# Modulation products as plain f32 matmuls on quarters of the array, half of them moved into block two, and an early gating of three retention heads

## The reference

```python
s_c = jax.nn.silu(c)
s_cc = jax.nn.silu(c_ctx)[None]
for i in range(DEPTH):
    ml = (s_c @ w_mod[i] + b_mod[i]).reshape(-1, 3, 3, D)     # for x
    mc = (s_cc @ w_mod[i] + b_mod[i]).reshape(-1, 3, 3, D)    # for the context
    h = gated_residual(h, ml, 0, swiglu(ada_in(h, norm_g[i, 0], ml, 0), ...), 0.5)
    xl = ada_in(h, norm_g[i, 1], ml, 1)      # then retention (i = 0) or neighbourhood attention (i = 1)
    h = gated_residual(h, ml, 1, yl, 1.0)
    h = gated_residual(h, ml, 2, swiglu(ada_in(h, norm_g[i, 2], ml, 2), ...), 0.5)
# ada_in: rms_norm(x) * (1 + m[:, j, 1]) + m[:, j, 0];  gated_residual: h + w * m[:, j, 2] * y
```

## Time and profile before

| | us |
|---|---|
| median of three runs | 3498.28 |
| lowest, highest | 3494.55, 3510.05 |
| the profiled execution, its span | 3498.12, 3496.3 |
| PE busy | 3340.3 (96%) |
| PEld, DVE, ACT, POOL busy | 2800.2, 1829.8, 1416.7, 93.1 |
| moved by DMA | 497.13 MB, 142 GB/s on average |

### The profile page before, as it was taken

One profiled execution on the slowest core, in us unless ns is written; L12 is line 12 of the kernel. 1 busy time (PEld: TensorE's weight loads), 2 busy tenths in 40 slices (PEclk: granted clock), 3 DMA queues, 4 the chain that ended last, 5 costly groups with the idle time before them and its releaser, 6 DMA issues.

```text
span 3496.3 us, 44481 instructions
## 1 busy us (share of the span) xinstructions
PE 3340.3 (96%) x17862; PEld 2800.2 (80%) x17862; DVE 1829.8 (52%) x2656; ACT 1416.7 (41%) x1898; POOL 93.1 (3%) x127
## 2 busy tenths in 40 slices
PE   7999979999999979999999999989999999999998
PEld 6888768888887768878888778768888788887797
DVE  6755666757756767753334343463333433344654
ACT  5644535545545435542222233233221322234543
POOL 0000000000000000000000000000000000021000
PEclk9999989999999989999999999999999999999999
DMA  7854426857754427843232222212333223254254
GB/s 242 275 186 158 151 77 199 266 196 258 254 169 152 135 96 229 265 157 97 97 112 99 85 85 85 84 49 97 97 103 103 87 98 110 91 133 100 76 181 156
DMA packets 354902, 497.13 MB, mean 142 GB/s; under 512 B 12658, under 2 KB 223500, under 8 KB 354700
## 3 DMA queue, kind: packets, MB, share of 16 engines
q1 hardware_dynamic: 351052, 483.76, 42.2%
q0 software_dynamic: 3648, 10.54, 1.4%
HBM read 493.16 MB, written 1.10 MB: 141 GB/s over the span
## 4 chain that ended last, share of the span: by engine, by line
PE 88%; DVE 6%; ACT 2%; issue 2%; POOL 1%; DMA 1%; SPq 0%; DVEq 0%; POOLq 0%; ACTq 0%
PE bank L483 27%; PE bank L484 26%; PE bank L485 26%; PE bank L496 2%; PE bank L498 2%; DVE wlo L1430 1%; PE bank L882 1%; ACT whi L1019 1%; DVE cv L1711 1%; DMA raw<-in_nat_w_qkv_dram 0%; PE bank L616 0%; PE bank L631 0%; POOL small L2174 0%; PE bank L867 0%; POOL small L2179 0%
## 5 line engine op out<-in xcount | busy, mean ns | idle before, releaser
L1430 DVE TENSOR_TENSOR wlo<-raw,whi 128x1024 fp32r<-128x1024 f32 (+1 forms) x926 | 1107.4, 1213 | 1263.4 <-ACT whi L1019 1262.1
L1019 ACT ACTIVATE whi<-raw 128x1024 fp32r<-128x1024 f32 (+1 forms) x926 | 953.3, 1047 | 1249.7 <-PE bank L485 1212.3
L483 PE MATMUL bank<-xTh,whi 128*128 128x256 f32 (+1 forms) x3200 | 1043.5, 326 | 9.4 <-ACT whi L1019 4.1
L484 PE MATMUL bank<-xTl,whi 128*128 128x256 f32 (+1 forms) x3200 | 1039.4, 325 | 0.0
L485 PE MATMUL bank<-xTh,wlo 128*128 128x256 f32 (+1 forms) x3200 | 1039.0, 325 | 0.0
L483 PEld LDWEIGHTS bank<-xTh,whi 128*128 128x128 f32 x3200 | 608.2, 190 | 72.7 <-issue 9.7
L484 PEld LDWEIGHTS bank<-xTl,whi 128*128 128x128 f32 x3200 | 608.4, 190 | 52.4 <-issue 0.5
L485 PEld LDWEIGHTS bank<-xTh,wlo 128*128 128x128 f32 x3200 | 607.8, 190 | 49.0
L483 PE MATMUL bank<-whi,hh 128*128 128x512 f32 x968 | 376.8, 389 | 0.0
L484 PE MATMUL bank<-wlo,hh 128*128 128x512 f32 x968 | 376.6, 389 | 0.0
L485 PE MATMUL bank<-whi,hl 128*128 128x512 f32 x968 | 376.6, 389 | 0.0
(11 more groups left out here) (331 smaller groups left out, 2485.0 us busy)
## 6 DMA issues: line engine op xcount, KB each, us to landing
raw<-in_ffn_w_in_dram SPq DMA_DIRECT2D x176, 1024.0 KB, 5.2
raw<-in_ffn_w_out_dram SPq DMA_DIRECT2D x80, 1024.0 KB, 5.1
raw<-in_w_mod_dram SPq DMA_DIRECT2D x72, 1024.0 KB, 5.2
raw<-in_w_in_dram SPq DMA_DIRECT2D x44, 1024.0 KB, 5.0
raw<-in_ret_w_in_dram SPq DMA_DIRECT2D x24, 1024.0 KB, 5.1
raw<-in_w_branch_dram SPq DMA_DIRECT2D x12, 1024.0 KB, 5.1
raw<-in_nat_w_qkv_dram SPq DMA_DIRECT2D x12, 1024.0 KB, 8.5
raw<-in_ffn_w_out_dram SPq DMA_DIRECT2D x16, 512.0 KB, 3.4
```

The lines of the kernel that those rows point to most:

```text
L483: pe.matmul(ps, lh, rh, start=start, stop=False, skip_group_check=True)
L484: pe.matmul(ps, lh, rl, start=False, stop=False, skip_group_check=True)
L1019: nc.scalar.activation(hi, src, ACT.Copy).then_inc(*e.inc("hi", key, part))
L1430: nc.vector.tensor_tensor(lo, src, hi.bitcast(F32), ALU.subtract).then_inc(*e.inc("lo", key, part))
```

## The change

The slabs of w_mod leave the common order. A new class `Modulation` lays them out: 12 batches of three modulations, six halves each. Each half is loaded as it is into one of four buffers `mraw` and multiplied unsplit, by plain f32 matmuls; each of the four 128-row pieces j of a half goes to columns 32j to 32j + 31 of the array, and so to partitions 32j and on of bank 7. The stationary side is a window of 32 columns of `scp`, which is zero but for two; the window is shifted by two columns for each modulation of a batch, so that a batch of three shares one bank. Six batches (one layer's) are in the FFNs of block one, six in the FFNs g1 and g2 of layer 0 and g1 of layer 1, all with T = 512. Four batches of block one have their last half at the end of the FFN (`END`). A batch's turn is one matmul with `sel` per 128 columns, which sums the four pieces at once. FFNs with modulations use seven banks. ACT copies the rows where DVE did. The gate rows of a layer are made in g1, whose group 9 turns them.

At the end of retention DVE gates and adds the sum of the first three heads beforehand (`three_heads`), and `rows` has only head 3's share left; ACT takes the split that followed `first_squares` ahead of it, DVE takes its own in the norm.

```diff
+MOD_BATCHES = {("f1", 0): (0,), ("f2", 0): (1, 2), ("f1", 1): (3, 4), ("f2", 1): (5,),
+               ("g1", 0): (6, 7), ("g2", 0): (8, 9), ("g1", 1): (10, 11)}
+MOD_POINTS = {1: (9, 13, 17, 21, 25, END), 2: (8, 10, 12, 14, 16, 18, 20, 22, 24, 26, 28, END),
+              512: (2, 3, 4, 5, 6, 7, 9, 9, 10, 11, 12, 13)}
...
+                        if wide:
+                            ahead = 3 if n < NMOD else at - 1
+                        else:
+                            ahead = 28 if at == END else max(6, at - (4 if len(batches) == 1 else 2))
+                        self.loads.setdefault(first + ahead, []).append(q)
...
                     sp.dma_start(view(raw[s % NRAW], key), src).then_inc(landed[s % NRAW], 16)
+                    for q in mods.loads.get(s, ()):
+                        name = mods.halves[q][4]
+                        if q >= NMOD:
+                            sp.wait_ge(*e.at("modk", q - NMOD))
+                        if name not in (("f1", 0), ("f1", 1), ("g1", 0)) and q < mods.first[name] + NMOD:
+                            sp.wait_ge(*e.at("turn", name, KD - 1))
+                        sp.dma_start(mraw[q % NMOD][:, :, :], mods.halves[q][3]).then_inc(mod_landed[q % NMOD], 16)
...
-                for part in range(2):
-                    wh, wl = split_ready(("mod", i, half), part)
-                    for j in range(2):
-                        k = 4 * half + 2 * part + j
-                        pe.matmul(ps[0:4, :], sc4[:, k, :], wh[:, j, :], start=k == 0, stop=False,
-                                  skip_group_check=True)
-                        m = pe.matmul(ps[0:2, :], sc4[:, k, 0:2], wl[:, j, :], start=False, stop=k == KD - 1,
-                                      skip_group_check=True)
...
+                ps = bank[MODS[0]]
+                pe.wait_ge(mod_landed[q % NMOD], 16 * (q // NMOD + 1))
+                for j in range(4):
+                    pm = pe.matmul(ps[32 * j:32 * j + 32, :], scp[:, 4 * half + j, 4 - 2 * m:36 - 2 * m], mraw[q % NMOD][:, j, :],
+                                   start=m == half == 0, stop=m == BATCH - 1 and half == 1, skip_group_check=True)
+                pm.then_inc(*e.inc("modk", q, also=[("modp", b)] if m == BATCH - 1 and half == 1 else []))
...
                 for c in range(4):
-                    m = pe.transpose(ps[:, 4 * c:4 * c + 4], modrow[0:4, c * P:(c + 1) * P], ident[0:4, 0:4])
-                m.then_inc(*e.inc("modtp", i))
+                    m = pe.matmul(ps[:, 6 * c:6 * c + 6], modrow[:, c * P:(c + 1) * P], sel, start=True, stop=True)
+                m.then_inc(*e.inc("modtp", b))
...
+                        mods_at(name, 2 * g + half)
...
+                        mods_at(name, 22 + 6 * n + d)
                 rows_by_tile([(name, "down", 1, d) for d in (4, 5)], ("down", name, 1), ps, *hv, k0, KF)
+                mods_at(name, END)
...
+                    if t == 0 and name in PREVIOUS:
+                        mod_rows(PREVIOUS[name], END)
...
+            def mod_rows(name, at):
+
+                if (name, at + 1) in mods.turns:
+                    b = mods.turns[name, at + 1]
...
+                    act.wait_ge(*e.at("modp", b))
+                    if b:
+                        act.wait_ge(*e.at("modtp", b - 1))
+                    A(modrow[:, :], unit("modp", b)[:, :], ACT.Copy).then_inc(*e.inc("modrow", b, frees=("modp", b)))
...
             ahead(until, ("rw", 3, 0))
+            ahead_of_tail(until, ("rw", 3, 1))
             first_squares(("g2", 0), 512)
-            ahead_of_tail(until, ("rw", 3, 1))
...
+            def gated(t, n, stage, key):
+
+                TT(stripe(X, n, t), stripe(X, n, t), stripe(Y, n, t), ALU.add).then_inc(*e.inc(stage, key, t, n))
+
+            def three_heads(t, n):
+                dve.wait_ge(*e.at("Y", 2, n, t))
+                dve.wait_ge(*e.at("gb", ("r",)))
+                TT(stripe(Y, n, t), stripe(Y, n, t), stripe(gbm, n, t // 2), ALU.mult).then_inc(*e.inc("Yg", 2, n, t))
+                dve.wait_ge(*e.at("Yg", 2, n, t))
+                gated(t, n, "X3", "r")
+
             def rows(t, n=1):
-                row(3, t, n)
-                dve.wait_ge(*e.at("Y", 3, n, t))
-                dve.wait_ge(*e.at("gb", ("r",)))
-                link(TT(stripe(Y, n, t), stripe(Y, n, t), stripe(gbm, n, t // 2), ALU.mult))
-                TT(stripe(X, n, t), stripe(X, n, t), stripe(Y, n, t), ALU.add)\
-                    .then_inc(*e.inc("X", ("g2", 0), t, n))
+                dve.wait_ge(*e.at("rwp", 3, n, t))
+                dve.wait_ge(*e.at("X3", "r", t, n))
+                TT(stripe(Y, n, t), unit("rwp", 3, n, t)[:, :], stripe(gbm, n, t // 2), ALU.mult)\
+                    .then_inc(*e.inc("Yg", 3, n, t, frees=("rwp", 3, n, t)))
+                dve.wait_ge(*e.at("Yg", 3, n, t))
+                gated(t, n, "X", ("g2", 0))
...
+            until(slabs.part_index[("rw", 3, 1), 0])
+            for t in range(4):
+                for n in range(2):
+                    three_heads(t, n)
             ahead(until, ("rw", 3, 0))
             for t in range(4):
                 rows(t, 0)
-            ahead_of_tail(until, ("rw", 3, 1))
             first_squares(("g2", 0), 512)
```

More of the change, by code:

```diff
@@ L135, in add, with __init__ @@
         self.items.append((key, src, kt, n, len(pieces)))
+class Modulation:
+    def __init__(self, slabs, w):
+        self.halves, self.uses, self.loads, self.turns, self.first, self.last = [], {}, {}, {}, {}, {}
+        for name, batches in MOD_BATCHES.items():
+            wide = name[0][0] == "g"
+            points = MOD_POINTS[512 if wide else len(batches)]
+            first = slabs.index[name, "gate", 0]
+            self.first[name], n = len(self.halves), 0
+            for b in batches:
+                for m in range(BATCH):
+                    l, g = divmod(BATCH * b + m, 18)
+                    for half in range(2):
+                        q, at = len(self.halves), points[n]
+                        src = w["w_mod_2"][l][512 * half:512 * half + 512, 512 * g:512 * g + 512]
+                        self.halves.append((b, m, half, src.rearrange("(k p) n -> p k n", p=P), name))
+                        self.uses.setdefault((name, at), []).append(q)
+                        if wide:
[3 more added lines that the diff above has]
+                        self.loads.setdefault(first + ahead, []).append(q)
+                        n += 1
+                self.turns[name, at + 1] = b
+            self.last[name] = len(self.halves) - 1
 def plan(w):
@@ L143, in rows, with ffn @@
         return m[k0 * P:(k0 + kt) * P, c0:c0 + n].rearrange("(k p) n -> p k n", p=P)
[L145 to L149, removed]
+    def ffn(name, w_up, w_down):
         for g in range(GROUPS):
@@ L223, in build @@
     slabs = plan(w)
+    mods = Modulation(slabs, w)
     with ExitStack() as ctx:
@@ L471, in new @@
             def new(*key, ring=ALL):
-                u = ring[L.units[ring] % len(ring)]
-                L.units[ring] += 1
+                turn = ALL if ring is SEVEN else ring
+                u = turn[L.units[turn] % len(turn)]
+                L.units[turn] += 1
+                if u not in ring:
+                    u = turn[L.units[turn] % len(turn)]
+                    L.units[turn] += 1
                 L.bank_of[key] = u
@@ L1100, in ffn @@
                         act.wait_ge(*e.at("ht", name, g, i))
-                        if name == ("g1", 0) and g + i == 0:
-                            act.wait_ge(L.sem("gate_rows_written"), 16 * DEPTH)
+                        if T == 512 and name in MOD_BATCHES and g == 7 and i == 0:
+                            act.wait_ge(*e.at("modk", mods.last[name]))
                         A(hh[:, o:o + 512], sg[:, b, :], ACT.Copy).then_inc(*e.inc("hhi", name, g, i))
-                    if mod0 is not None and 0 < g <= MODS_PER_FFN:
-                        ahead(until, ("mod", mod0 + g - 1, 1))
+                    mod_rows(name, 2 * g + 1)
+                    if g == 9 and name in GATES_OF:
+                        l = GATES_OF[name]
+                        act.wait_ge(*e.at("growp", l))
+                        A(grow, unit("growp", l)[0:48, 0:P], ACT.Copy).then_inc(*e.inc("grow", l, frees=("growp", l)))
                 for n in range(2):
```

206 lines of the change are left out of this document (112 added, 94 removed).

## The result

The changed kernel takes 3473.89 us (median of four runs, 3471.68 to 3477.20) against 3500.24 us for the kernel before on the same chip: ratio 0.9928, 95% interval 0.9914 to 0.9942, 26.4 us less. The forecast was 3432, 66 us less, with 3414 to 3496 as its range. The time fell, as forecast, and lies in the range, but 26 of the 66 us came.

What follows compares the result with a forecast made beforehand. It took the kernel as PE-bound. From 3498.1 us: -148.7 for today's modulation, +74.8 halves, +10.4 turns, +3.0 late squares, -5.3 end of retention, together -65.8, giving 3432; range 3414 to 3496.

Steps and rivals of the forecast that it cites:

- What hides the rest: Splits, row copies, loads and seven banks stay hidden behind PE; a lost cover would stall one to two us per FFN.
- the price of going in and out of a block: Entering and leaving a block of quarter matmuls adds 0.24 us to 0.86, making a half 1.10 us.
- two at a time: Rival: only two f32 streams fit at once, a half takes 1.96 us, total time 3494 us; chance 12%.
- The modulation now and its turns: On PE, 72 halves and 36 turns cost 148.7 us before; twelve turns of 0.87 us, 10.4 us, after.
- the two rivals on the quarters: Quarter matmuls start strictly as issued (3525 us, chance 10%) or only two go side by side (3494 us, chance 12%).
- strict order: Rival: matmuls start strictly as issued, a half takes 2.39 us, total time 3525 us; chance 10%.
- The four halves at the end of FFNs: In block one, halves put where PE idles delay ACT's squares by 0.75 us each, 3.0 us in all.
- The end of retention: Gating three heads early on DVE makes the last xn start earlier, 5.3 us less, bounds 0 and 9.5.
- With seven banks in place of eight a bank is wanted again after most of two groups' work: In FFNs with modulations, each bank is read long before it is wanted again, so no cost was counted.

Runs made afterwards that it cites:

- e2: The changed kernel with small tables laid into free columns of cols, so the activation arrays lie where they lay before the change: 3460.36 us, ratio 0.9892.
- e3: The kernel before with only the early gating of three heads at the end of retention and the two moved splits: 3494.52 us, ratio 0.9989.
- e12: e5 with the end of retention put back as in the kernel before, so the modulation part alone: 3456.01 us, ratio 0.9877.
- e5: e2 with four banks of the ring skipped once ahead of the neighbour attention: 3452.9 us, ratio 0.9874.
- e6: e5 with the ring of banks also set to its old point at the start of both mixers: 3459.19 us, ratio 0.9889.
- e11: e5 with nine f32 matmuls on constants filling PE's wait for the rotated queries in both mixers: 3447.06 us, ratio 0.9851.
- e1: The kernel before with 320 bytes of empty space ahead of the activation arrays, nothing else changed: 3521.8 us, ratio 1.0064.

## Why the prediction missed

The step that failed is "What hides the rest": it puts everything outside the terms of the sum at nothing, and the runs show 12.6 us for the place of the arrays and some 6 for the ring of banks there. Beside it one term, the price of going in and out of a block, was too small by 6.8 us, and the mixers lost 16 us to a half clock whose cause is open. That the time lies in the range is luck: the forecast's own range ended at 3456, and it was stretched to 3496 for the rival of two at a time, which did not come.

**The modulation now and its turns: right.** Neither of the two rivals on the quarters came: four streams run side by side, no strict order and no limit of two. The twelve turns cost 0.81 us in the timeline and some 0.1 behind, for 0.87 forecast. The two FFNs of block one with twelve halves are 23.2 and 21.4 us shorter in the profile of e2, for 23 forecast; the 21.4 hold 0.8 of late squares behind f2.

**Going in and out of the block: too small.** The forecast took 0.86 + 0.24 us for a half; the first term stands (0.85 measured by itself), the second is 0.34. 68 times 0.10 us are 6.8 us. The way out was read from a block that changes between other shapes, and the way in was put at half of it by guess. The Trainium skill, "TensorEngine Tiling (Array Packing)", Key Properties, says that a change of tiling mode drains the engine. This trace agrees in so far as the change has a price, 0.34 us there and back; not all of it need be the change of shape, for the late next matmul (0.10 of the 0.34) stands with 0.08 also behind a turn, which keeps the shape 128*128. In the FFNs of 512 rows, 12 halves in 11 blocks and two turns should then make 16 us for the 15 forecast; in e2 the three are 19.0, 14.2 and 16.5 us longer, and the 14.2 holds the 1.9 that e3 gained there.

**The four halves at the end of FFNs: right.** ACT reads the bank first and starts the squares late. PE's timeline at the turn of xn behind f1, after and before, beside the earlier trace rows:

```profile
216.75 1.06 PE L544 MATMUL bank<-mraw,scp 128*32 128x512 f32 x8
218.08 0.63 PE L674 MATMUL bank<-cst,xn 128*128 128x128 f32 x4 [0.27 <-DVE xn L1553]
220.48 1.20 PE L674 MATMUL bank<-cst,xn 128*128 128x128 f32 x9 [1.77 <-DVE xn L1553]
```

```profile
251.50 1.53 PE L616 MATMUL bank<-cst,xn 128*128 128x128 f32 x12 [0.98 <-DVE xn L1475]
```

The second tiles come 2.40 us behind the first in place of 1.61 (249.89 to 251.50), 0.8 us for the 0.75 forecast.

**The end of retention: right** in the profile: 12.2 us from product to FFN matmul for 12, and 6.4 us less in the retention and the FFN behind it (e3) for 5.3. The runs have 3.8, with an interval from 9 less to 1 more. Beside the shorter list of DVE there is a gain that the forecast didn't count: at this place the granted clock is at 0.50 for 13.7 us in the kernel before and in e12, and for 6.8 us in e3 and in the changed kernel.

**"With seven banks in place of eight a bank is wanted again after most of two groups' work": failed.** It weighs what seven banks do inside an FFN, and there nothing happened. It doesn't look at where the ring stands when the FFN is over. In the neighbour attention, right behind the last FFN with seven banks, it cost a wait of 4.9 us, 6.3 us by the ratios of e2 and e5, whose intervals overlap.

**"What hides the rest" left out the table sizes: failed.** The two kernels show them (`cst` shorter, `scp` new, `scc`, `sc4` and `modt` gone), and nothing in the sum stands for them. They moved the activations by 320 bytes, and 12.6 us went there, by the ratios. This is the largest cause that the runs show, and no row of the profile before could have priced it; but the kernels showed that the arrays move, and the range could have said so.

**The mixers.** 19.4 us more in the profile of e5; two turns (1.8) and two late squares (1.6) were in the sum, the other 16 go with the half clock. The two mixers of e5 stand at 0.50 for 24 and 27 us more than before; at 26 matmuls in place of 37 in the same time this costs 15 us. In all seven profiles with the new modulation the mixer of layer 0 takes 313 to 316 us; in six of seven without it, 304 to 307, in one (e3) 311.4. In layer 1 it is 306.8 to 314.0 against 303.8 to 307.0. That the change brings it on more often is seen; by which way is open. Banks (e6), placement (e2 has it at the old place) and the end of retention (e12) are not it, and the fill of e11 did not settle it. Nor does it need the new modulation: e3, with 311.4, has the same piece of 30.7 us.

Against the 39 us that were missing on the runs stand 12.6 for the place, 6.3 for the ring, 6.8 for the half, and 16 for the clock in the mixers, the last from single profiles. The sum goes by way of e5: the profile of the changed kernel itself has the long half clock in layer 0 alone, and part of what the old place gave was lost to it in layer 1. That these are 42 and not 39 is within what single profiles leave, such as the neighbour attention, 3.8 us shorter in e5 than before.

## What to carry to other kernels

A block of four f32 quarter matmuls costs two records (0.86 us at 512 columns) and 0.34 us of going in and out; put several halves in one block and the 0.34 are paid once. When a diff resizes any static table, compute where the arrays behind it land and compare the distance between matmul operands before and after; keep it, or measure the new one. And when a stage takes fewer buffers out of a ring, follow the ring's phase into every later stage that mixes it with fixed buffers.

## What the runs showed of the hardware

The place of the activations in SBUF relative to the arrays ahead of them, the split weights among them, changes the pace of fp32r matmuls: 226 to 227 ns at 512 columns where it is as before or 256 bytes more, 229 to 236 ns where it is 64, 128 or 320 bytes more (medians by operands; one group of e1, `xTh` with `wlo`, stays at 226). At 256 columns the median start-to-start falls from 120 to 117 or 118 ns with 64 or 320 bytes more. The Trainium skill, "TensorE: Matmul & The Clock Gate", Part 2, says that the streaming operand and the weight load have independent read ports, so that loading the next weights takes nothing from the running matmul; here, with a weight load for each matmul, the pace depends on how the arrays lie to each other, by up to 9 ns in 227. The measurement decides that there is such a dependence; no run shows that the weight load is what takes the time.

Plain f32 matmuls on four different column quarters start their first records within 0.02 us of each other, ahead of the second records of those issued earlier. The granted clock in the attention of the mixer falls to 0.50 for 30.7 us in one piece in some kernels and for 7 to 10 in others, with the same instructions; nine filling matmuls ahead of it (e11) left the 30.7 us of layer 0 as they were.
